# Hybrid diffusion step in fp32 on one core: the scan's inverse on 32x32 blocks with DVE's block transpose, and the prompt's expert rows handled for eight experts at once

## What is computed

```python
h = rmsnorm(x) * (1 + sc1) + sh1
proj = h @ w_in
# a: RWKV-7, 8 heads x 64, forward and backward in time
#   s = s * w_t + (s @ -kk_t) (kk_t * a_t)^T + v_t k_t^T ;  y_t = s @ r_t
# b: neighbourhood attention (sample), full attention (prompt), 8 heads x 64
x = x + gt1 * (concat(ya, yb) @ w_out)
h = rmsnorm(x) * (1 + sc2) + sh2
aff = softmax(h @ router)                 # 16 experts
gate, idx = top_k(aff.T, cap)             # cap = 128 sample rows, 16 prompt rows per expert
xe = h[idx]
ye = (silu(xe @ e_gate) * (xe @ e_up)) @ e_down * gate      # D_EXPERT = 2816
x = x + gt2 * scatter_add(idx, ye)
```

## Time and profile before

| | us |
|---|---|
| median of 3 runs | 3862.87 |
| lowest and highest run | 3862.14, 3871.79 |
| the profiled execution's own time | 3860.96 |
| its span, first to last instruction | 3859.2 |
| TensorE busy with matmuls | 3562.1 (92%) |
| DVE busy | 1231.4 (32%) |
| ScalarE busy | 671.1 (17%) |

### The profile page before, as it was taken

One profiled execution on the slowest core, in us unless ns is written; L12 is line 12 of the kernel. 1 busy time (PEld: TensorE's weight loads), 2 busy tenths in 40 slices (PEclk: granted clock), 3 DMA queues, 4 the chain that ended last, 5 costly groups with the idle time before them and its releaser, 6 DMA issues. The chain is left out here.

```text
span 3859.2 us, 81746 instructions
## 1 busy us (share of the span) xinstructions
PE 3562.1 (92%) x37038; PEld 3101.1 (80%) x37038; DVE 1231.4 (32%) x3103; ACT 671.1 (17%) x1677; POOL 192.0 (5%) x150
## 2 busy tenths in 40 slices
PE   5899899999899979289999999999999999999995
PEld 2387685959555545189999999999999999999995
DVE  3376767777444443701111111111111111111112
ACT  2323324242144532100000000000000000000001
POOL 0010101010000000000000000000000000000000
PEclk7899999999999999589999999999999999999997
DMA  7200000000121022098887878788787878878773
GB/s 323 61 16 10 15 5 20 4 19 4 27 79 31 18 72 94 21 354 292 274 266 263 267 259 273 261 273 268 265 267 258 273 262 269 268 268 269 258 251 110
DMA packets 498393, 664.38 MB, mean 172 GB/s; under 512 B 31183, under 2 KB 437095, under 8 KB 494975
## 3 DMA queue, kind: packets, MB, share of 16 engines
q1 hardware_dynamic: 492238, 640.23, 49.5%
q0 software_dynamic: 5632, 18.88, 1.9%
q10 hardware_dynamic: 176, 0.05, 0.0%
HBM read 630.70 MB, written 28.36 MB: 171 GB/s over the span
## 5 line engine op out<-in xcount | busy, mean ns | idle before, releaser
L2094 PE MATMUL bank<-e_hid,e_wd 128*128 128x144 f32 x5632 | 760.1, 288 | 0.0
L2082 PE MATMUL bank<-e_xT,e_wg 128*128 128x144 f32 x5632 | 749.5, 286 | 1.0 <-ACT e_xT L2136 1.0
L2082 PE MATMUL bank<-e_xT,e_wu 128*128 128x144 f32 x5632 | 748.1, 286 | 0.0
L2082 PEld LDWEIGHTS bank<-e_xT,e_wg 128*128 128x128 f32 x5632 | 715.5, 190 | 1.0 <-issue 1.0
L2094 PEld LDWEIGHTS bank<-e_hid,e_wd 128*128 128x128 f32 x5632 | 710.5, 190 | 5.6
L2082 PEld LDWEIGHTS bank<-e_xT,e_wu 128*128 128x128 f32 x5632 | 714.4, 190 | 0.0
L2179 DVE TENSOR_TENSOR e_tm<-bank,e_sg 128x144 f32<-128x144 f32 x352 | 108.3, 308 | 1853.0 <-ACT e_sg L2143 1853.0
L2143 ACT ACTIVATE e_sg<-bank 128x144 f32<-128x144 f32 x352 | 102.2, 290 | 1998.4 <-PE bank L2082 1998.4
L532 PE MATMUL bank<-hT_x,wblk 128*128 128x512 f32 (+1 forms) x672 | 237.5, 511 | 14.5 <-DMA wblk<-in_w_in 8.5
L532 PEld LDWEIGHTS bank<-hT_x,wblk 128*128 128x128 f32 x672 | 114.1, 197 | 130.4 <-issue 112.4
L727 PE MATMUL bank<-r_TW,r_X 64*64 64x64 f32 x2880 | 167.5, 220 | 4.3 <-DVE r_X L1198 1.3
(11 more groups left out here) (324 smaller groups left out, 3469.9 us busy)
## 6 DMA issues: line engine op xcount, KB each, us to landing
e_wg<-in_e_gate SPq DMA_DIRECT2D x176, 1024.0 KB, 5.5
e_wu<-in_e_up SPq DMA_DIRECT2D x176, 1024.0 KB, 8.1
e_wd<-in_e_down SPq DMA_DIRECT2D x176, 1024.0 KB, 11.0
h_wmod<-in_w_mod SPq DMA_DIRECT2D x24, 1024.0 KB, 17.1
wblk<-in_w_in SPq DMA_DIRECT2D x22, 512.0 KB
h_x<-in_x_sample SPq DMA_DIRECT2D x8, 512.0 KB, 6.6
wo<-in_w_out SPq DMA_DIRECT2D x2, 2048.0 KB, 11.6
o_x<-in_x_sample SPq DMA_DIRECT2D x8, 512.0 KB, 4.2
```

The source lines that it names most:

```text
L2082: last = nc.tensor.matmul(bank[6 + b % 2][:, j * TOK:(j + 1) * TOK], w[s][:, k, f], xT[e % 2][:, k, :], start=(k == 0), stop=(k == KD - 1))
L2094: last = nc.tensor.matmul(bank[k // PER_BANK][:, c:c + TOK], wd[s][:, b % DUO, k * P:(k + 1) * P], hid[:, b % 2, :], start=(b == 0 and k % ...
```

## The change

In the scan the inverse is made on the four diagonal 32x32 blocks of a pair's partitions (`QS`), in levels 1 to 4; T0 comes from DVE's block transpose instead of TensorE and ScalarE. The last doubling, from 32 to 64, is done for W alone: `last_X` and `last_Y` fill the off-diagonal blocks of a new tile `WF`, which state_U then reads. M_products places its blocks so that M's own diagonal and off-diagonal 32x32 blocks lie on the partitions where they are used. In the experts the prompt's rows of eight experts are gathered at once (128 rows), transposed in 8 transposes, and copied by DVE into each expert's xT; the results are collected by DVE into `ypT`, turned back for eight (then seven) experts at once, scaled at once and scattered expert by expert; expert 15 is turned back alone. Top-k does the prompt first, and SP rewrites the prompt's lists through DRAM meanwhile. The core of the diff:

```diff
 def rwkv(K, A):
-    LV = 5
+    LV = 4
-        TW = [sb(f"TW{i}", [P, 2, 2, 2, CH]) for i in range(2)]
+        TW = [sb(f"TW{i}", [P, 2, 2, 2, HB]) for i in range(2)]
+        WF = [sb(f"WF{i}", [P, 2, 2, CH]) for i in range(2)]
...
             @block.tensor
                     def M_products(g, d):
                         for i in range(2):
-                            at = piece(d, 2 * g + i)
-                            for q, src in enumerate((B[d], KB[d])):
-                                for hs in HS:
-                                    last = nc.tensor.matmul(bank[d][hs, (2 * i + q) * P:(2 * i + q + 1) * P],
-                                                            src[hs, at], QR[d][hs, :, at], start=True, stop=True)
+                            at, c = piece(d, 2 * g + i), 2 * i * P
+                            for h, hs in enumerate(HS):
+                                for b in range(2):
+                                    rows = QS[2 * h + b]
+                                    own, other = at.start + b * HB, at.start + (1 - b) * HB
+                                    nc.tensor.matmul(bank[d][rows, c:c + HB], B[d][hs, own:own + HB],
+                                                     Q[d][hs, own:own + HB], start=True, stop=True)
+                                    nc.tensor.matmul(bank[d][rows, c + HB:c + CH], B[d][hs, own:own + HB],
+                                                     Q[d][hs, other:other + HB], start=True, stop=True)
+                            for hs in HS:
+                                nc.tensor.matmul(bank[d][hs, c + CH:c + P], B[d][hs, at], R[d][hs, at],
+                                                 start=True, stop=True)
+                            for hs in HS:
+                                last = nc.tensor.matmul(bank[d][hs, c + P:c + 2 * P], KB[d][hs, at], QR[d][hs, :, at],
+                                                        start=True, stop=True)
...
-                    def inverse_start(g):
...
                     def level_X(g, lev):
...
-                                for hs in HS:
-                                    last = nc.tensor.matmul(bank[2 + d][hs, i * CH:(i + 1) * CH],
-                                                            M[g % 3][hs, d, i, 0, 0:CH], TW[g % 2][hs, d, 0, i, :],
+                                for qs in QS:
+                                    last = nc.tensor.matmul(bank[2 + d][qs, i * HB:(i + 1) * HB],
+                                                            M[g % 3][qs, d, i, 0, 0:HB], TW[g % 2][qs, d, 0, i, :],
...
+                    def last_X(g):
+                        pe.wait_ge(tw_ok, p * (GR * NTW) + (g + 1) * NTW)
+                        for i in range(2):
+                            for d in range(2):
+                                for h in range(2):
+                                    src, to = QS[2 * h + d], QS[2 * h + 1 - d]
+                                    last = nc.tensor.matmul(bank[2][to, i * HB:(i + 1) * HB],
+                                                            M[g % 3][src, d, i, 0, HB:CH], TW[g % 2][src, d, 0, i, :],
+                                                            start=True, stop=True)
+                        last.then_inc(xlps, 1)
+                    def last_Y(g):
+                        pe.wait_ge(xl_ok, p * GR + g + 1)
...
+                                    last = nc.tensor.matmul(bank[5][to, CH + i * HB:CH + (i + 1) * HB], XL[src, i, :],
+                                                            TW[g % 2][src, d, 1, i, :], start=True, stop=True)
...
                     for g in range(GR + 1):
                         j = 2 * (g - 1)
-                        if g < GR:
-                            inverse_start(g)
-                            level_X(g, 1)
                         if g:
+                            last_X(g - 1)
                             state_Z(j)
...
                             M_products(g + 1, 0)
+                        if g:
+                            last_Y(g - 1)
                         if g < GR:
-                            level_Y(g, 1)
+                            level_X(g, 1)
...
                             M_products(g + 1, 1)
+                        if g:
+                            pe.wait_ge(wf_ok, p * GR + g)
+                        if g < GR:
+                            level_Y(g, 1)
...
                         if g < GR:
+                            PV_KV(g)
                             level_X(g, 4)
                         if g:
                             state_S(j + 1)
                         if g < GR:
                             level_Y(g, 4)
-                            PV_KV(g)
-                            level_X(g, 5)
-                            level_Y(g, 5)
             @block.scalar
+                    def last_X(g):
+                        act.wait_ge(xlps, p * GR + g + 1)
+                        nc.scalar.activation(XL[:, :, :].rearrange("p i t -> p (i t)"), bank[2][:, 0:CH], ACT.Copy,
+                                             scale=-1.0).then_inc(xl_ok, 1)
+                        for q, qs in enumerate(QS):
+                            b = q % 2
+                            nc.scalar.activation(WF[g % 2][qs, :, :, b * HB:(b + 1) * HB], TW[g % 2][qs, :, 1, :, :], ACT.Copy)
+                    def last_Y(g):
...
+                        for q, qs in enumerate(QS):
+                            d = q % 2
+                            last = nc.scalar.activation(WF[g % 2][qs, d, :, (1 - d) * HB:(2 - d) * HB], 
+                                                        bank[5][qs, CH:P].rearrange("p (i t) -> p i t", t=HB), ACT.Copy)
+                        last.then_inc(wf_ok, 1)
             @block.vector
...
                     def inverse_start(g):
...
+                        dve.wait_ge(w0_ok, p * GR + g + 1)
+                        for d in range(2):
+                            V.transpose(TW[g % 2][:, d, 0, :, :].rearrange("p i t -> p (i t)"),
+                                        TW[g % 2][:, d, 1, :, :].rearrange("p i t -> p (i t)")).then_inc(t0_ok, 1)
 def topk(K, A):
...
+            @block.sync
+            def _(sp):
+                sp.wait_ge(prompt_ok, 1)
+                sp.dma_start(K.dram["idxq"][:, :], idx[:, CAP:TOK]).then_inc(listed, 16)
+                sp.dma_start(K.dram["gateq"][:, :], val[:, CAP:TOK]).then_inc(listed, 16)
+                sp.wait_ge(listed, 32)
+                for dst, name in ((K.idxq, "idxq"), (K.gateq, "gateq")):
+                    sp.dma_start(dst[:, :], bass.AP(tensor=K.dram[name].tensor, offset=0, ap=[[1, P], [P, 2]]),
+                                 allow_slow_non_contiguous=True).then_inc(loaded, 16)
...
-                for at, n, col, cap in ((0, NS, 0, CAP), (NS, NP, CAP, CAPP)):
+                for at, n, col, cap in ((NS, NP, CAP, CAPP), (0, NS, 0, CAP)):
 def experts(K, A):
...
             @block.gpsimd
...
                 gather(0)
+                gather_prompt(0)
...
+                    for g, (first, last) in enumerate(GROUP):
+                        if e == last + 1 or (e == last and last == NE - 1):
+                            K.hold(pool, sp_ok, 2 * g + 2)
+                            for i in range(first, last):
+                                scatter_prompt(i)
...
+                K.hold(pool, sp_ok, 6)
+                scatter_prompt(NE - 1)
             @block.tensor
...
-                    last = nc.tensor.transpose(bank[b][:, c + CAP:c + TOK], xp[:, k * P:(k + 1) * P],
-                                               K.ident[0:CAPP, 0:CAPP])
...
-                    last = nc.tensor.transpose(bank[5][0:CAPP, c], yT[:, k, CAP:TOK], K.ident[:, :])
...
+                        if e == GROUP[0][1] - 1 and b in (2, 3, 4, 5, 9, 10, 11, 12):
+                            prompt_token(1, b - 2 if b < 6 else b - 5, 5)
+                        for g, (first, last) in enumerate(GROUP):
+                            if e == last and b in (4, 5, 6, 7, 10, 11, 12, 13):
+                                prompt_output(g, b - 4 if b < 8 else b - 6)
             @block.vector
...
+                    V.tensor_copy(xT[e % 2][:, :, CAP:TOK], xpT[:, :, part(e)]).then_inc(xv_ok, 1)
...
+                    V.tensor_copy(ypT[:, :, part(e)], yT[:, :, CAP:TOK]).then_inc(yc_ok, 1)
...
+                        if e == GROUP[0][1] - 1 and b in (8, 15):
+                            prompt_tokens(1, b // 15, 5)
+                        for g, (first, last) in enumerate(GROUP):
+                            if e == last and b in (9, 15):
+                                prompt_scaled(g, b // 15)
```

More of the change, by code:

```diff
@@ L34 @@
 CH = 64
+HB = CH // 2
 CHUNKS = NT // CH
@@ L420, in rwkv @@
         HS = [slice(h * HN, (h + 1) * HN) for h in range(2)]
+        QS = [slice(q * HB, (q + 1) * HB) for q in range(4)]
         bank = K.bank
@@ L691, in PV_KV @@
                         last.then_inc(kvps, 1)
-                    def inverse_start(g):
```

(18 more changed lines are left out.)

238 lines of the change are left out of this document (160 added, 78 removed).

## The result

| | before | after |
|---|---|---|
| median of the runs, us | 3863.11 | 3976.35 (ratio 1.028, 95% interval 1.026 to 1.030) |
| span of the profiled execution | 3859.2 | 3965.7 |
| matmul records on TensorE | 37038 | 45462 |
| from the first matmul of the experts to the last | 2166 | 2109 |
| from the first scan group to the last | 770 | 939 |

The forecast was 3833, range 3770 to 3895. The time fell outside on the slow side: the experts gave what they should, and the scan, put at +22 us, cost some 170.

The account below looks back on a forecast made before the run. The prediction took TensorE to bound both the scan and the experts. From 3862.9 us it added 22 for the scan, took off 53 for the experts and added 1.5 at their start: 3833 us, range 3770 to 3895.

Parts of the forecast that it names:

- the scan's sum: Scan group: stream 10.7, shape changes 2.8, last_X wait 1.8, other waits 0.6, less 0.3 overlap: 15.6 us, +22 us in all.
- the clock: Scan and experts: the granted clock was taken to stay at 1.00, so nothing was added for it.
- The step that priced a 32x32 matmul at 0.016 us: Scan's inverse: four tiles overlap in waves, cost scaling with columns; 208 matmuls take 3.3 us a group, bounds 0.012 and 0.058 each.
- The slower rivals built on dearer small matmuls: Scan: a wave of four keeps 0.058 us, total 3912, 13%; or every record takes 0.029 us, total 4095, 4%.
- 22.9 us a group (4095): Rival for the scan: every record takes 0.029 us, so 208 matmuls take 12.1 us a group; +284 us, 4%.
- 25 ns between starts: Scan: the skill's least gap between matmul starts, making 416 records 10.4 us and the total near 4030; no separate chance given.
- M_products: Scan: a piece goes from 0.44 us to 0.69, four take 2.75 us a group against 1.75.
- Change of shape: Scan: 23 changes of tile shape a group at 0.12 us each, 2.8 us; bounds 0 and 0.15 each.
- The wait ahead of last_X: Scan: TensorE waits 1.8 us a group for DVE, whose small pairs were taken at 0.44 us each.
- ScalarE's copies are covered: Scan: ScalarE loses two copies and gets nine, 1.3 and 0.9 us, hidden beside state_Z and M_products.
- Experts: Experts: fewer prompt and token transposes save 53 us; at their start the wait changes by 0 to +3, taken +1.5.
- The head, top-k and gt2p: Around the scan and experts: extra constants, the prompt lists' small DMAs and gt2p's 128-row load were taken to cost nothing.

Follow-up runs that it names:

- bf16_twice: Kernel after with the whole inverse in bf16 and every wave of four of its matmuls issued twice, to the same result: 3970.4 us, ratio 1.027.
- level_X_bf16: Kernel after with level_X alone reading the upper halves of its fp32 values as bf16: 3909.2 us, ratio 1.012.
- T_by_dve: Kernel after in fp32, with level_Y making only W's sum on TensorE and DVE's block transpose making T after every level: 3882.2 us, ratio 1.005.
- T_by_dve_natural_order: T_by_dve with M_products and the causal mask of the kernel before, and N0 made in four quarters: 3842.0 us, ratio 0.994.
- inverse_bf16: Kernel after with the inverse's matmuls (level_X, level_Y, last_X, last_Y) reading upper halves as bf16, one pass each: 3797.9 us, ratio 0.982.
- experts_only: Kernel before with the change's top-k and experts alone, head and scan as before: 3806.0 us against 3864.9, ratio 0.9846.
- (a): Stream of bench_tiles: fp32 32x32 matmuls in waves of four, 1024 matmuls, no waits inside: 56.1 us.
- bench_tiles: Kernel before with an added stage after top-k: five TensorE streams without waits inside, 4096 instructions each; run once, (a) took 56.1 us.
- stream (e): Stream of bench_tiles: eight 32x32 and eight 64x64 matmuls of 128 columns in turns, 64 times; a turn took 1.28 us.
- experts_and_bf16_64: experts_only with level_X and level_Y of the old 64x64 scan reading upper halves as bf16: 3736.8 us, ratio 0.966.
- scan_only: Kernel before with the change's head, scan and their constants alone, top-k and experts as before: 4035.9 us, ratio 1.0435.
- Stream (c): Stream of bench_tiles: fp32 64x64 matmuls with 32 columns, 4096 instructions, no waits inside: 109.3 us at a clock of 0.50.
- (b): Stream of bench_tiles: fp32 64x64 matmuls with 64 columns, 4096 instructions, no waits inside; expected 59 us, granted clock 0.97.

## Why the prediction was wrong

All kernels in one table, with the supply a group needs at 3.74 us for 256 instructions:

| | instructions a group | supply, us | group, us (its mean clock) | groups at 0.97 or more, us | time, us |
|---|---|---|---|---|---|
| after | 1344 | 19.6 | 19.7 (0.88) | 19.4 | 3976 |
| bf16_twice | 1344 | 19.6 | 19.9 (0.72) | none | 3970 |
| level_X_bf16 | 1216 | 17.8 | 18.0 (0.87) | 17.2 | 3909 |
| T_by_dve | 1088 | 15.9 | 17.1 (0.84) | 16.2 | 3882 |
| T_by_dve_natural_order | 960 | 14.0 | 16.0 (0.90) | 14.8 | 3842 |
| inverse_bf16 | 928 | 13.6 | 15.0 (0.86) | 13.7 | 3798 |
| experts_only (old scan) | 864 | 12.6 | 15.0 (1.00) | 15.0 | 3806 |

The group columns are means over the 28 full groups of one profiled execution.

**The step that failed** is the scan's sum itself: "10.7 + 2.8 + 1.8 + 0.6 - 0.3 = 15.6 us". For what it counts the sum holds: the eleven groups of after at full clock take 15.4 us once their stops are taken out. Yet a group takes 19.7, because the sum holds only what the array and the waits do. It has no line for what the stream consumes, 1344 instructions at 3.7 us for 256. A second term was put at nothing with little reason, the clock ("I leave it there"). In after the supply hides it almost wholly, but not in the versions that need fewer instructions. The step that priced a 32x32 matmul at 0.016 us was right, and it is what made the supply bind: at 8 ns a record, 4 ns an instruction, a wave uses up instructions over three times as fast as they come (14.6 ns). The kernel before stood close to that edge already: 864 instructions in 15.0 us, 17.4 ns each. The trace of before could have told half of it: 16 KB packets of q8, three in the group of the earlier trace rows (four with q14). That one fetch has to be over before the next makes way, and takes 3.74 us, no row of it shows.

The Trainium skill (Runtime: NRT & Kernel Launch, Instruction fetch mechanics) has the blocks of 16 KiB, 256 instructions, that the stops show. It calls the cost of crossing a boundary mostly hidden, since instructions are dispatched slower than they are fetched. The runs here say otherwise for small matmuls: stops of 1.3 to 2.5 us at every block in (a), 3.4 us a group in the scan.

Point by point:

- *Waves:* 0.016 us, confirmed. The slower rivals built on dearer small matmuls named the right side with a cause that was not there. 22.9 us a group (4095) came from the assumption that records can't start so close; they do, for as long as there are instructions.
- *25 ns between starts* (the Trainium skill, TensorE: Matmul & The Clock Gate, "Wait — 56ns, not 53.3ns?"), by which the prediction's estimate was 4030, names the right side and is nearer to 3976 than the forecast, but by accident: the rows at 263.12 have starts 8 ns apart in a long run, on different tiles.
- *M_products:* 0.69 a piece and its share of changes, 0.90 together; measured 0.76 (270.12 to 270.88). The seven changes of columns alone are cheaper than I took them, or overlap.
- *Change of shape:* 0.12 taken, 0.14 measured (bench_tiles, stream (e)).
- *The wait ahead of last_X:* 1.8 forecast; 1.10 at most in after, 1.48 in inverse_bf16. My 0.44 for each small pair on DVE was high:

```profile
266.99 0.35 DVE L1231 TENSOR_TENSOR r_N<-r_M,level 128x64 f32<-128x64 f32 x2
267.38 0.36 DVE L1238 TENSOR_TENSOR r_TW<-r_N,id 128x64 f32<-128x64 f32 x2
267.77 0.37 DVE L1242 STREAM_TRANSPOSE r_TW<-r_TW 128x64 f32<-128x64 f32 x2
```

- *ScalarE's copies are covered:* nearly; in the waits of the scan TensorE's for r_WF come to 7.3 us in all (4.7 ahead of state_U, 2.6 ahead of level_Y).
- *The clock:* "I leave it there" was wrong. In all 28 full groups of before the granted clock is 1.00; over the scan of after it is 0.88. It is not the cause of the 171 us: at full clock a group still takes 19.4 of the 19.7 us, and stream (a) stops as often with the array idle for nearly half of it. A lower clock doesn't need the stops either: experts_and_bf16_64 has none, and half of its groups were granted 0.87 to 0.89. And it would have cost without them: after's groups less their stops are 16.8 us on average, and 15.4 at full clock, an estimate from the traces by subtraction. Why it falls in the new scan and not in the old one stays open.
- *Experts:* -53 and +1.5 taken, -59 measured. (The 55.8 in that sum is 55.2 when redone; it changes nothing.) An expert's period is 131.1 as forecast, and from the first product with weights to the last down(e, b) the stage is 54.2 us shorter in experts_only. The start was forecast at 0 to +3 and is -1.6: from the turning of the lists to that first product it takes 16.1 us (1642.67 to 1658.76), 17.7 before (1638.49 to 1656.15), as eight pairs of token transposes became two runs of eight. From the last down(e, b) to the end 4.7 us go. Behind the last transpose 40.4 us are left for 43.0; a prompt's scatter by itself lands in 3.4 us and not the 6.3 of my estimate. (The profiled execution of experts_only starts top-k 4.1 us later than that of before, 1578.08 for 1574.01, after code that is the same; starts may not be compared across the two.)
- *The head, top-k and gt2p* at nothing: right for two of them by the traces. DVE's last addition of the head ends 0.1 us later in after (81.95 for 81.83), and from top-k's first maximum to the turning of the lists it takes 64.6 us for 64.5. gt2p by itself was not measured. experts_only and scan_only add up to the whole within 1 us, so no cost of either hides in the other.

**What to carry to other kernels.** Before cutting work into more and smaller matmuls, count TensorE's instructions (two for a bf16 matmul, four for fp32) against the stage's time: where the stage leaves less than 15 ns for each on average, or 24 ns beside DMA at 407 GB/s (figures of these runs), supply is the bound, and a saving in array time buys nothing. The sign in a profile is "issue" idle in the middle of runs, at a fixed count of instructions and on no fixed line. To cut the count, use larger tiles, fewer passes, or move transposes to DVE. Then read the granted clock group by group: once supply no longer binds, a clock below 1.00 is paid in full (13.7 and 16.7 us in inverse_bf16). And experts_only shows that dropping the part that breaks the budget can beat both kernels.

## What the runs showed that was not expected

- TensorE takes about 522 instructions without a stop after pauses of 6.6 to 11.5 us, then 256 in some 3.5 to 3.8 us with DMA quiet (single blocks 3.3 to 4.0), and in 6.21 us at 407 GB/s.
- A 64x64 fp32 matmul costs 0.058 us with 64 columns, 0.055 with 32, 0.109 with 128: below 64 columns its price stays. Four 32x32 tiles with 32 columns do scale, 0.016 each.
- Stream (c) kept TensorE busy for all of its 109 us and was granted 0.50 (1.2 GHz) throughout; (b), the same with 64 columns, 0.97.
